# One attention step with a merged value product and the scaling moved to GpSimd, in a one-core streaming-encoder kernel

## What is computed

```python
h = rmsnorm(x, g_norm1)
qa, ka, va, qb, kb, vb, gates = split(h @ w_in)
# branch A, per chunk of 64 rows, 8 heads on 2 K/V heads, window 128 + own chunk
s = qa . ka * 64**-0.5 + bias                 # T5 relative bias
p = softmax(concat([s, sink]))[..., :-1]      # a learned sink per head
oa = p . va
# branch B, stick breaking, strictly causal, 8 heads
z = qb . kb * 64**-0.5
log_1m = where(mask, log_sigmoid(-z), 0)
tail = reversed_cumsum(log_1m) - log_1m
ob = where(mask, exp(log_sigmoid(z) + tail), 0) . vb
merged = sigmoid(gate_a) * (oa @ w_proj_a) + sigmoid(gate_b) * (ob @ w_proj_b)
x = x + merged @ w_out
x = x + square(relu(rmsnorm(x, g_norm2) @ w_up)) @ w_down
y = rmsnorm(x, g_final)
```

## Time and profile before

| what | value |
|---|---|
| median of 3 runs | 863.22 us (862.98 to 863.53) |
| the profiled execution | 863.73 us |
| its span, first to last instruction | 861.9 us |
| granted TensorE clock, mean | 0.991 |
| busy share PE, PEld, DVE, ACT, POOL | 97%, 94%, 74%, 44%, 34% |
| DMA moved | 78.17 MB |

### The profile page before, as it was taken

The page is one execution under the profiler, slowest core; times in us unless marked ns, Lnnn a source line. Parts: engine busy times, 40 slices in busy tenths (PEclk is TensorE's granted clock), DMA queues, the critical chain, the costliest instruction groups (busy, mean ns, idle before and its releaser), DMA issues.

```text
span 861.9 us, 15995 instructions
## 1 busy us (share of the span) xinstructions
PE 832.4 (97%) x6197; PEld 812.0 (94%) x6197; DVE 641.1 (74%) x1103; ACT 383.2 (44%) x638; POOL 294.9 (34%) x213
## 2 busy tenths in 40 slices
PE   6999999999999999999999999999999999999994
PEld 4999999999899989899999999999999999999994
DVE  5778887344698898968335889479884889488995
ACT  5545666142457686653343333333332333333431
POOL 2553222311644455425434500443016400552330
PEclk9999999999999999999999999999999999999997
DMA  7761210632111111223321311431133312422203
GB/s 220 241 194 57 65 61 20 205 122 87 50 51 49 49 49 49 70 86 150 123 89 59 98 49 55 143 98 53 56 101 133 97 49 89 127 76 82 64 1 110
DMA packets 67392, 78.17 MB, mean 91 GB/s; under 512 B 2520, under 2 KB 62992, under 8 KB 66960
## 3 DMA queue, kind: packets, MB, share of 16 engines
q1 hardware_dynamic: 66912, 76.40, 27.8%
q10 hardware_dynamic: 432, 1.11, 0.3%
HBM read 70.15 MB, written 8.93 MB: 92 GB/s over the span
## 4 chain that ended last, share of the span: by engine, by line
PE 86%; DVE 10%; issue 1%; ACT 1%; DMA 1%; ACTq 0%; DVEq 0%
PE pan L1429 55%; PE pan L1607 13%; PE att L1607 11%; PE att L1471 1%; PE att L1545 1%; DVE sp_lo L1087 1%; DVE sp L1081 1%; PE att L1518 1%; DVE sp_hi L1085 1%; DVE sp L1076 1%; PE att L1535 1%; DMA x_rows<-in_x_prompt 1%; DVE sp_lo L1150 1%; PE att L1685 1%; DVE m_a L1115 0%
## 5 line engine op out<-in xcount | busy, mean ns | idle before, releaser
L438 POOL TENSOR_TENSOR w_lo<-raw,w_hi 128x512 fp32r<-128x512 f32 x164 | 226.8, 1408 | 459.8 <-ACT w_hi L759 182.3
L1429 PE MATMUL pan<-a_hi,w_hi 128*128 128x288 f32 x672 | 146.5, 300 | 0.0
L1429 PE MATMUL pan<-a_lo,w_hi 128*128 128x288 f32 x672 | 144.5, 297 | 0.0
L1429 PE MATMUL pan<-a_hi,w_lo 128*128 128x288 f32 x672 | 144.5, 297 | 0.0
L1429 PE MATMUL pan<-h_hi,w_hi 128*128 128x288 f32 x512 | 110.0, 296 | 0.0
L1429 PE MATMUL pan<-h_hi,w_lo 128*128 128x288 f32 x512 | 109.7, 295 | 0.0
L1429 PE MATMUL pan<-h_lo,w_hi 128*128 128x288 f32 x512 | 109.7, 295 | 0.0
L1429 PEld LDWEIGHTS pan<-a_hi,w_hi 128*128 128x128 f32 x672 | 108.2, 190 | 1.6 <-POOL w_lo L438 1.3
L1429 PEld LDWEIGHTS pan<-a_hi,w_lo 128*128 128x128 f32 x672 | 108.9, 190 | 0.0
L1429 PEld LDWEIGHTS pan<-a_lo,w_hi 128*128 128x128 f32 x672 | 108.7, 190 | 0.0
L1607 PE MATMUL pan<-F_hi,w_hi 128*128 128x288 f32 x320 | 95.4, 298 | 0.0
(11 more groups left out here) (244 smaller groups left out, 1737.2 us busy)
## 6 DMA issues: line engine op xcount, KB each, us to landing
raw<-in_w_in SPq DMA_DIRECT2D x34, 512.0 KB, 4.8
raw<-in_w_up SPq DMA_DIRECT2D x32, 512.0 KB, 4.7
raw<-in_w_down SPq DMA_DIRECT2D x32, 512.0 KB, 4.7
raw<-in_w_out SPq DMA_DIRECT2D x8, 512.0 KB, 4.1
x_spill<-xT SPq DMA_DIRECT2D x1, 2304.0 KB, 11.3
xT<-x_spill SPq DMA_DIRECT2D x1, 2304.0 KB, 10.8
x_rows<-in_x_prompt SPq DMA_DIRECT2D x2, 1024.0 KB, 6.9
raw<-in_w_pa SPq DMA_DIRECT2D x4, 512.0 KB, 4.5
```

Source lines behind the costliest of these rows:

```text
L438: last = nc.gpsimd.tensor_tensor(w_lo[:, slot, k:k + 4, :], raw[:, rs, k:k + 4, j * P:(j + 1) * P], w_hi[:, slot, k:k + 4, :].bitcast(F32) ...
L1429: got = nc.tensor.matmul(out[:, h, 0:HALF], w, x[:, h * HALF:(h + 1) * HALF], start=first and n == 0, stop=last and n == 2)
```

## The change

1. The sink goes into the row reduction: DVE computes the negated sum and takes the minimum starting from -sink, straight into `negm`. `mx`, the two small instructions and their semaphores go. ACT takes exponentials with scale -1, and the sinks with two instructions instead of one.
2. `normalise` moves from ACT to POOL as two `tensor_scalar` instructions; POOL's loop of splits is written out, with `normalise(g+1)` ahead of the splits of tile g.
3. `values(g)` loads both parts of V as 128 weight columns: two matmuls for a key block instead of three, into 128 partitions. The upper 64 hold the lo part; ACT's new `take_low(g)` copies them to SBUF behind `exps(g+2)` and behind a rounding of weights. DVE `outputs(g)` waits for that copy, adds it to the lower half into `oa_f`, rounds `oa_f` to `oa_hi` and subtracts to `oa_lo`.
4. Sample unit scores: the four cache blocks stand between the four steps of the first half panel. In u = 0 all sums come before `take_proj(0)` and all splits behind; in u = 1 `take_proj(4)` comes before the third bank.
5. Gate products: for i = 2, 3 one stands ahead of the last `sp_lo`, two behind `take_gate`; one each goes to the end of (1, 1) and (2, 1).

```diff
+            def split_at(n):
...
+            for n in range(2, 10):
+                split_at(n)
+            normalise(0)
+            split_at(10)
+            for g in range(SW_TILES):
+                if g + 1 < SW_TILES:
+                    normalise(g + 1)
+                for before, steps in ((SW_LEAD + 3 * g - 1, 1), (SW_LEAD + 3 * g, 2)):
+                    ended = sw_ended(before, steps)
+                    if ended:
+                        split_at(ended + 4)
...
+                pool.wait_ge(rden_ready, g + 1)
+                for e in range(2):
+                    last = nc.gpsimd.tensor_scalar(s_sw[0:w, r, e, ks], s_sw[0:w, r, e, ks], rden[0:w, r, e:e + 1], None, ALU.mult)
...
+            def take_low(g):
+
+                w = width(SW_ORDER[g % 5])
+                act.wait_ge(swo_out, g + 1)
+                nc.scalar.activation(va_low[:, :, 0:w], att[HD:P, 3, 0:2 * P].rearrange("p (e n) -> p e n", e=2)[:, :, 0:w], ACT.Copy).then_inc(va_low_out, 1)
...
                 ended = sw_ended(SW_LEAD + 3 * g, 2)
                 if ended:
                     round_at(ended + 4)
+                take_low(g)
...
-                        in1=bias[0:w, 2 * pair + e, ks], scale=1.0, scalar=NEG, op0=ALU.add, op1=ALU.max,
-                        accum_out=mx[0:w, r, e:e + 1])
+                        in1=bias[0:w, 2 * pair + e, ks], scale=-1.0, scalar=nsink[0:w, 2 * pair + e:2 * pair + e + 1], op0=ALU.add, op1=ALU.min,
+                        accum_out=negm[0:w, r, e:e + 1])
...
-                dve.wait_ge(swo_out, g + 1)
+                own = oa_f[:, g % 2, 0:w]
+                dve.wait_ge(va_low_out, g + 1)
+                if g >= 2:
+                    dve.wait_ge(oa_split, g - 1)
                 for e in range(2):
-                    last = nc.vector.tensor_copy(oa_hi[e * HD:(e + 1) * HD, pair, c0:c0 + w], att[0:HD, 3, e * P:e * P + w])
-                last.then_inc(swo_hi, 1)
+                    last = nc.vector.tensor_tensor(oa_f[e * HD:(e + 1) * HD, g % 2, 0:w], att[0:HD, 3, e * P:e * P + w],
+                                                   va_low[:, e, 0:w], ALU.add)
+                last.then_inc(swo_taken, 1)
+                dve.wait_ge(swo_taken, g + 1)
+                nc.vector.tensor_copy(oa_hi[:, pair, c0:c0 + w], own).then_inc(swo_hi, 1)
                 dve.wait_ge(swo_hi, g + 1)
+                nc.vector.tensor_tensor(oa_lo[:, pair, c0:c0 + w], own, oa_hi[:, pair, c0:c0 + w].bitcast(F32),
+                                        ALU.subtract).then_inc(oa_split, 1)
...
-                terms = [(*block, *parts) for block in key_blocks(t) for parts in ((0, pT_hi), (0, pT_lo), (1, pT_hi))]
+                terms = [(*block, part) for block in key_blocks(t) for part in (pT_hi, pT_lo)]
...
+                if u == 0:
+                    for n in range(3):
+                        added = sb_add(u, n, SAMPLE_ORDER, SAMPLE_W, SAMPLE_ADDS, added)
+                    dve.wait_ge(vrows_out, TT + 1)
+                    take_proj(0)
+                    for n in range(3):
+                        sb_split(u, n, SAMPLE_ORDER, SAMPLE_W)
...
                         if i >= 2:
-                            for t in range(4 * i - 8, 4 * i - 5):
-                                gate_m(t)
+                            gate_m(4 * i - 7)
...
                     if q == 0 and i >= 2:
+                        gate_m(4 * i - 6)
                         gate_m(4 * i - 5)
+                    elif q and i in (1, 2):
+                        gate_m(4 * i - 4)
...
+                def blocks_between(k):
+
+                    sample_block(u, (2, 3, 0, 1)[k])
+                    if u == 0 and k == 2:
+                        v_rows(3)
+
+                half_panel(18 + 2 * u, 0, slot4(2 * u), oa_hi, oa_lo, middle=blocks_between)
```

More of the change, by code:

```diff
@@ L137, in build @@
         ka_lo = work("ka_lo", [P, KVH, KEYS], 86016, F32R)
+        oa_f = work("oa_f", [P, 2, P], 78336)
+        va_low = work("va_low", [HD, 2, P], 79360)
         va_st = work("va_st", [P, 6, KVH, 2, HD], 91648, F32R)
@@ L457, in stage_low, with normalise @@
                 pool.wait_ge(kq_ready, i * 2 + (q + 1))
-            with pool.Fori(0, 5) as b:
-                split_body(b, range(4))
+            def split_at(n):
+                split(n % 4, n // 2 % 2, n % 2, n + 1)
+            def normalise(g):
+                t, r = SW_ORDER[g % 5], g % 2
+                w, ks = width(t), sw_cols(t)
+                pool.wait_ge(rden_ready, g + 1)
+                for e in range(2):
+                    last = nc.gpsimd.tensor_scalar(s_sw[0:w, r, e, ks], s_sw[0:w, r, e, ks], rden[0:w, r, e:e + 1], None, ALU.mult)
+                last.then_inc(p_ready, 1)
+            for n in range(2, 10):
[9 more added lines that the diff above has]
+                        split_at(ended + 4)
+            for n in range(18, 22):
+                split_at(n)
             split_body(5, (0, 1, 2))
@@ L584, in exps @@
                 w, ks = width(t), sw_cols(t)
[L585 removed]
+                pair = g // 5
+                act.wait_ge(max_ready, g + 1)
                 for e in range(2):
[L587 removed]
+                    nc.scalar.activation(s_sw[0:w, r, e, ks], s_sw[0:w, r, e, ks], ACT.Exp, bias=negm[0:w, r, e:e + 1], scale=-1.0,
                                          accum_out=den[0:w, r, e:e + 1])
[L589 to L595 removed]
                 for e in range(2):
[L597 to L598 removed]
+                    last = nc.scalar.activation(snk[0:w, r, e:e + 1], nsink[0:w, 2 * pair + e:2 * pair + e + 1], ACT.Exp, bias=negm[0:w, r, e:e + 1], scale=-1.0)
+                last.then_inc(exp_ready, 1)
             def take_pT(g):
@@ new lines, in sb_add @@
+            def sb_add(u, n, order, wid, adds, added):
+                bank, w = order[n], wid[order[n]]
+                cs = slice(BANK[bank], BANK[bank] + w)
+                dve.wait_ge(l_ready, u * 3 + (n + 1))
+                nc.vector.scalar_tensor_tensor(out=sp[:, cs], in0=att[:, BANK[bank] // 512, 0:w], scalar=0.0, in1=sp[:, cs],
+                                               op0=ALU.max, op1=ALU.add).then_inc(sp_ready, 1)
+                dve.wait_ge(sp_ready, u * 3 + (n + 1))
+                for to, late, w in adds[bank]:
+                    added += 1
+                    nc.vector.tensor_tensor(sp[:, to:to + w], sp[:, to:to + w], sp[:, late:late + w], ALU.add).then_inc(sp_added, 1)
+                    dve.wait_ge(sp_added, adds_before(u) + added)
+                return added
@@ new lines, in sb_split, with sb_sums @@
+            def sb_split(u, n, order, wid):
+                cs = slice(BANK[order[n]], BANK[order[n]] + wid[order[n]])
+                nc.vector.tensor_copy(sp_hi[:, cs], sp[:, cs]).then_inc(sp_hi_ready, 1)
+                dve.wait_ge(sp_hi_ready, u * 3 + (n + 1))
+                nc.vector.tensor_tensor(sp_lo[:, cs], sp[:, cs], sp_hi[:, cs].bitcast(F32), ALU.subtract).then_inc(sp_split, 1)
+            def sb_sums(u, order, wid, adds):
+                added = 0
+                for n in range(3):
+                    added = sb_add(u, n, order, wid, adds, added)
+                    sb_split(u, n, order, wid)
@@ L1095, in _ @@
                 magnitudes(u, SAMPLE_ORDER, SAMPLE_W)
-                sb_sums(u, SAMPLE_ORDER, SAMPLE_W, SAMPLE_ADDS, between=lambda: take_proj(4 * u))
+                added = 0
+                if u == 0:
[3 more added lines that the diff above has]
+                    take_proj(0)
+                    for n in range(3):
+                        sb_split(u, n, SAMPLE_ORDER, SAMPLE_W)
+                else:
+                    for n in range(3):
+                        if n == 2:
+                            take_proj(4)
+                        added = sb_add(u, n, SAMPLE_ORDER, SAMPLE_W, SAMPLE_ADDS, added)
+                        sb_split(u, n, SAMPLE_ORDER, SAMPLE_W)
                 for n in range(1, 4):
@@ L1615, in sample_scores, with sample_block @@
                 got.then_inc(z_out, 1)
-                for kbs in ((2, 3), (0, 1)):
-                    for kb in kbs:
-                        bank, c = SAMPLE_KB[kb]
-                        for h in range(4):
-                            got = acc(att[:, bank, c % 512 + h * NEW:c % 512 + (h + 1) * NEW], cKT[rows, h, kb * P:(kb + 1) * P],
-                                      qkvT[rows, QB + h, SEQ:TOK], start=kb % 2 == 0 and h == 0, stop=kb % 2 == 1 and h == 3)
+            def sample_block(u, kb):
+                rows = slice(u * HD, (u + 1) * HD)
+                bank, c = SAMPLE_KB[kb]
+                for h in range(4):
+                    got = acc(att[:, bank, c % 512 + h * NEW:c % 512 + (h + 1) * NEW], cKT[rows, h, kb * P:(kb + 1) * P],
+                              qkvT[rows, QB + h, SEQ:TOK], start=kb % 2 == 0 and h == 0, stop=kb % 2 == 1 and h == 3)
+                if kb % 2:
                     got.then_inc(z_out, 1)
```

62 lines of the change are left out of this document (10 added, 52 removed).

## The result

The changed kernel takes 887.39 us (median of 4 runs, 886.13 to 887.54), the kernel before beside it 863.38 (862.98 to 864.43): a ratio of 1.0271 (1.0253 to 1.029), slower. The profiled execution has a span of 885.7 us and a mean granted clock of 0.980.

The account below looks back on a forecast made before the run. PE, busy 97%, bounds the kernel; after the change a DVE-ACT loop paces the attention stage. 863.7 + 12.5 (attention) + 0.1 (sample) - 1.9 (gates) = 874.4, median 0.5 lower: 873.9 us, range 865 to 882.

Parts of the forecast that it names:

- PE's saving: Attention stage: fewer value matmuls take 4.0 us off PE, counting only if PE still sets the pace.
- The new loop: Attention stage: outputs waits for take_low on ACT; 4.31 us per 256-column tile, 78.4 us for the stage before rounds and splits.
- the ring: Attention stage: the serial path from one pT_low to the next through DVE and ACT, claimed longer than PE's work.
- Rounds and splits: Attention stage: ACT's rounding or take_qkv and POOL's splits lengthen the loop at seven panels, 13.7 us in all.
- The last hand-over: End of the attention stage: the last pT_low distance, one loop less 0.95 because no exponentials are ahead.
- the third rival: Attention stage: normalising pairs over 3 us on POOL and a clock falling to 1.2 GHz; about 881, chance 0.15.
- the rival's other half: Attention stage: a POOL normalising pair over 3 us, lengthening every loop; the main forecast took 0.64 per instruction.
- Sample part: Two sample units: new V-row waits against removed half-clock stretches and waits, +1.1 and -1.0, together +0.1 us.
- the range's upper end: Sample part: +3 us if the clock falls within the 3.2 us wait for V rows.
- Gates: Gate units (2, 0) and (3, 0): waits of 3.9 us vanish, half given back, -1.9 us.
- Port-free: Attention stage: DVE and POOL do not hold each other, so 7.5 us goes; 866.4 us, chance 0.15.
- PE-bound: Attention stage: the loop fits in PE's 3.7 us a tile, so the kernel gets faster; 853 us, chance 0.1.

Follow-up runs that it names:

- e9: Kernel before with the sink in the row minimum alone: 862.0 us, ratio 0.9967.
- e11: The best guess without the sample part, and VectorE instead of GpSimd does the attention stage's seven splits: 860.13 us, ratio 0.9933.
- e3: Changed kernel with take_low(g) ahead of the rounding of weights, not behind it: 882.0 us, ratio 1.0209.
- e6: Changed kernel; in the first sample unit ScalarE takes all V cache rows ahead of the second bank's exponentials: 883.03 us, ratio 1.0228.
- e4: Changed kernel with the scaling of the value rows back on ScalarE instead of GpSimd: 886.2 us, ratio 1.0266.
- e12: Kernel before with VectorE's half of the sample part alone (order of sums, splits and take_proj): 859.63 us, ratio 0.9949.
- e13: Kernel before with TensorE's half of the sample part alone (cache blocks between panel steps, V rows behind them): 869.78 us, ratio 1.0067.
- e7: Kernel before with the gate products spread over the columns alone: 860.36 us, ratio 0.996.
- e15: Kernel before with the sink in the row minimum, VectorE's sample order without the cache blocks between steps, and the gate products spread: 854.02 us, ratio 0.988.
- e14: Kernel before with the sink in the row minimum and the gate products spread: 857.94 us, ratio 0.9926.
- e8: Kernel before with the whole sample part of the change alone: 868.05 us, ratio 1.0059.
- the best guess: Changed kernel, but VectorE copies the low half, ScalarE does the scaling, V rows come ahead of the second bank's exponentials: 862.68 us, ratio 1.0001.

## Why the prediction was wrong

The direction and the mechanism held, the size did not: +10.7 was forecast, +24.0 came, and 887.4 lies above the range's 882. In the span: stage +22.3 for +12.5, sample part +5.2 for +0.1, gates -2.85 for -1.9. Two steps failed: the sum for one tile of the new loop, 4.31 where it measures 4.77, with the last hand-over and the clock on top of it; and the sample part, put at nothing in sum.

**PE's saving** is real and, as said, of no use: the loop sets the pace.

**The new loop: the terms of ScalarE and of the reductions were too small.** The sum for a tile with 256 columns was 4.31. In the rows above it is: `pT_low` and reductions 1.51 (1.41 forecast: each reduction, now with a pointer for its start value, takes 0.48 instead of 0.41); exponentials and two sink steps 85.67 to 87.16, 1.49 (1.18: the second sink step was priced at 0.09 from an instruction with 2 columns and no bias; the pair of one column with bias pointers takes 0.47); copy 0.41 (0.41); additions 0.62 (0.61); cast and subtraction 0.47 (0.43); denominator 0.27 (0.27). That is 4.77. The hand-over shown is 4.90, as its `pT_lo` came another 0.13 later, behind transposes that ran at half clock; the next one of the same kind is 4.78. The other kinds run 4.23, 4.52 and 4.52 where 3.81, 4.05 and 4.07 stood. Twelve ordinary hand-overs miss 5.6 together, 0.41 to 0.60 each. The dearer steps matter because they stand in the ring: in e9, outside it, they cost nothing.

**Rounds and splits.** Five long hand-overs were forecast at 6.2 to 6.8 and are 6.6, 6.6, 6.4, 6.4 and 6.8. That is luck: the tile under them was priced too low and the collision too high (the extra was 2.1, not 2.45), and the two errors nearly cancel, 0.1 over each. The prediction writes that the Trainium skill speaks against this part; it is the other way round, its rule is the one that the part uses. That a VectorE step with two SBUF inputs stands under a split, as the Trainium skill says (SBUF — State Buffer, "Who interferes with whom"), agrees with 1.25 for 0.29, and e11 confirms it from the other side: without GpSimd's split the step takes 0.29 again.

**Two sizes that the sum lacked.** The last hand-over was taken at 3.1, the loop less 0.95 of exponentials; it is 4.91. The loop through ScalarE no longer sets it: PE's values, one panel step and the transposes do, and PE ran at half clock there. Part of the miss is not the clock's: the kernel before took 3.56 for this hand-over at full clock, and e3, at full clock, 4.27, with the scaling late behind a split. In the changed kernel:

```profile
167.55 0.58 PE L1587 MATMUL att<-pT_hi,va_st 128*128 128x256 f32 x1 [3.25 <-DVE pT_lo L1021]
...
168.14 0.41 PE L1587 MATMUL att<-pT_hi,va_st 128*128 128x256 f32 x1
...
170.01 1.05 PE L1577 MATMUL att<-ident,s_sw 128*128 128x128 f32 x4
```

Products that start 0.12 apart at full clock start 0.21 apart here. And the hand-over of tile 11 is 5.47 at half clock; the same one in e6, at full clock, is 4.50. Against the 4.05 and 3.1 of the forecast that is 1.4 and 1.8, together 3.2. By the full-clock values, 4.50 and 3.56, the clock's share of it is about 2.3, an estimate. The clock was part of the third rival ("about 881"), with one microsecond for each of several tiles, and it cost about that in two; the rival's other half, a slow pair on GpSimd, did not come true: the pair takes 1.83, not 1.28 as assumed and not over 3, and e4 shows it costing nothing.

The twelve, the five and these two make 5.6 + 0.5 + 1.4 + 1.8 = 9.3 of the stage's miss of 9.8.

**Sample part.** The wait for V rows was forecast as 3.2 and is 2.95. Wrong were three things. The forecast counted on 1.7 in each unit from a clock that panel steps between the blocks would keep up. Nothing of this 3.4 came: as much time as before, 6.83 us, ran at half clock, from 211.2 on, which is within the wait for V rows, where the range's upper end had placed it; and in e6 the clock fell among the blocks themselves. The blocks were taken to cost the same apart as in one piece, and cost 1.2 a unit more. And the second unit was to gain 1.0: it is 26.33 instead of 25.48, with waits of 1.41 and 1.44 for the copy and the split sums. The step also priced TensorE's half and VectorE's half together, and so hid that VectorE's alone gains 4.8 us and TensorE's alone costs 5.4 (e12, e13).

**Gates.** The waits of the earlier trace rows are gone, as forecast. Half of their 3.9 was given back for collisions that did not come in that size; 2.85 came, inside the range. e7 shows it alone.

**Rivals.** Port-free (866.4) and PE-bound (853) are refuted: the step is held for 1.25, and the ring is longer than PE's work. That e15 takes 854.0 says nothing for the 853, which counted on 4.0 of matmuls that e15 does not save.

## What to carry to other kernels

When an engine in the loop begins to wait for another one, price every step of that other engine's list up to the signal, from rows of the exact form: a second small instruction counted 0.09 was 0.28. Work removed from PE, which the loop did not wait for, brought nothing here. GpSimd's added scaling cost nothing while the ring was longer (e4), and 4.4 us once the ring was gone. And a change of several parts is to be priced, and tried, part by part: here five parts made +24 us, while the sink, the gates and VectorE's half of the sample part alone made -10. Parts in different stages added up (e14, e15); the two halves of the sample part, which share one, did not (e12, e13, e8).

## What the runs showed of the hardware

- The half clock also comes without a gap. In e15 the second sample unit has PE busy all of its 25.05 us, at a granted clock of 0.86; in e12 the same instructions, as gapless, have 1.00 and take 22.12. So 2.9 us of one unit are the clock's alone, and where the stretches fall differs between kernels with the same code there.
- While GpSimd splits, VectorE's steps with two SBUF inputs stand: 1.21 to 1.39 us instead of 0.15 to 0.29 in the best guess. So does its 128x128 cast from SBUF to SBUF, 1.31 instead of 0.23 at 125.86 there. None is held where VectorE does the split itself (e11).
- Two small exponentials, 128x1 with pointers for bias, take 0.47 together; one of 128x2 without them 0.19.
- GpSimd multiplies 128x256 by a column in 0.93 us and 64x192 in 0.76; in the kernel before ScalarE does the two of 128x256 in 0.91 together.
- A block of eight 64-column products with a full-width panel step on either side costs 0.3 us more than its share of one long piece: 1.03 for 0.93 in the block, 0.99 for 0.79 in the step behind it, at full clock.
